# Up-projection of a layer started on the scaled residual, before the root of its norm is known

## The reference

```
x = x + merged @ w_out[l]
h = rms_norm(x, norm_ffn[l])              # x * rsqrt(mean(x*x) + EPS) * gain
ff_g, ff_u = jnp.split(h @ ffn_up[l], 2, axis=-1)
ff_g = causal_dwconv(ff_g, ffn_conv_w[l], ffn_conv_b[l])      # three taps along the tokens
x = x + (jax.nn.gelu(ff_g) * ff_u) @ ffn_down[l]
```

## Time and profile before

| | us |
|---|---|
| median of three runs | 3583.91 (3582.96 to 3587.26) |
| the profiled execution, its own time | 3586.41 |
| its span, first to last instruction | 3584.6 |
| PE busy | 3518.6 |
| DVE busy | 2136.5 |
| ACT busy | 1397.5 |

### The profile page before, as it was taken

One profiled execution on the slowest core, in us unless ns is written; L12 is line 12 of the kernel. 1 busy time (PEld: TensorE's weight loads), 2 busy tenths in 40 slices (PEclk: granted clock), 3 DMA queues, 4 the chain that ended last, 5 costly groups with the idle time before them and its releaser, 6 DMA issues. The chain is left out here.

```text
span 3584.6 us, 53211 instructions
## 1 busy us (share of the span) xinstructions
PE 3518.6 (98%) x21547; PEld 2874.6 (80%) x21547; DVE 2136.5 (60%) x3001; ACT 1397.5 (39%) x1599; POOL 0.2 (0%) x4
## 2 busy tenths in 40 slices
PE   8999999999999999999999999999999999999998
PEld 6778778887877787788878778988888778878887
DVE  6888565876368885658763657653233667652233
ACT  6465433433254554334432334233222443332223
POOL 0000000000000000000000000000000000000000
PEclk9999999999999999999999999999999999999999
DMA  4222222554232222225542331132222330133321
GB/s 130 80 83 60 83 94 98 197 197 154 88 93 75 76 66 83 94 95 200 196 155 84 94 129 49 50 107 94 94 94 86 103 129 26 61 106 98 101 94 70
DMA packets 273304, 364.38 MB, mean 102 GB/s; under 512 B 22637, under 2 KB 218977, under 8 KB 271841
## 3 DMA queue, kind: packets, MB, share of 16 engines
q1 hardware_dynamic: 247856, 311.34, 27.2%
q10 hardware_dynamic: 25264, 50.43, 4.0%
HBM read 351.79 MB, written 9.96 MB: 101 GB/s over the span
## 5 line engine op out<-in xcount | busy, mean ns | idle before, releaser
L249 PE MATMUL banks<-act_hi,w_hi 128*128 128x512 f32 x4064 | 1607.8, 396 | 21.8 <-issue 6.1
L251 PE MATMUL banks<-act_hi,w_lo 128*128 128x512 f32 x4064 | 1584.4, 390 | 0.0
L250 PE MATMUL banks<-act_lo,w_hi 128*128 128x512 f32 x4064 | 1583.4, 390 | 0.0
L171 DVE TENSOR_TENSOR w_lo<-w_raw,w_hi 128x2048 fp32r<-128x2048 f32 (+1 forms) x280 | 629.1, 2247 | 637.9 <-ACT w_hi L165 633.4
L249 PEld LDWEIGHTS banks<-act_hi,w_hi 128*128 128x128 f32 x4064 | 763.3, 188 | 217.6 <-issue 46.7
L251 PEld LDWEIGHTS banks<-act_hi,w_lo 128*128 128x128 f32 x4064 | 762.5, 188 | 162.3
L250 PEld LDWEIGHTS banks<-act_lo,w_hi 128*128 128x128 f32 x4064 | 763.2, 188 | 158.8 <-issue 3.8
L165 ACT ACTIVATE w_hi<-w_raw 128x2048 fp32r<-128x2048 f32 (+1 forms) x280 | 526.5, 1881 | 909.5 <-PE banks L251 845.8
L2127 DVE SCALAR_TENSOR_TENSOR arena<-arena,small 128x512 f32<-128x512 f32 x168 | 126.3, 752 | 12.9
L249 PE MATMUL banks<-w_hi,act_hi 128*128 128x256 f32 x384 | 111.0, 289 | 3.6 <-DVE w_lo L171 3.6
L250 PE MATMUL banks<-w_lo,act_hi 128*128 128x256 f32 x384 | 109.3, 285 | 0.0
(11 more groups left out here) (388 smaller groups left out, 3385.1 us busy)
## 6 DMA issues: line engine op xcount, KB each, us to landing
w_raw<-in_w_in SPq DMA_DIRECT2D x98, 1024.0 KB, 5.5
w_raw<-in_ffn_up SPq DMA_DIRECT2D x48, 1024.0 KB, 5.4
arena<-in_ada_w ACTq DMA_DIRECT2D x24, 2048.0 KB, 8.1
w_raw<-in_w_gu SPq DMA_DIRECT2D x44, 1024.0 KB, 5.1
w_raw<-in_ffn_down SPq DMA_DIRECT2D x24, 1024.0 KB, 5.0
w_raw<-in_w_down SPq DMA_DIRECT2D x20, 1024.0 KB, 4.9
w_raw<-in_w_out SPq DMA_DIRECT2D x16, 1024.0 KB, 4.9
w_raw<-in_w_branch SPq DMA_DIRECT2D x12, 1024.0 KB, 5.0
```

The source lines that it names most:

```text
L171: self.core.nc.vector.tensor_tensor(view(self.lo[:, s]), view(self.raw[:, s]), view(self.hi[:, s]).bitcast(FP32), ALU.subtract)\
L249: nc.tensor.matmul(out, wh, ah, start=first, stop=False)
L250: nc.tensor.matmul(out, wh, al, start=False, stop=False)
L251: return nc.tensor.matmul(out, wl, ah, start=False, stop=last)
```

## The change

- **Outer.plain** takes the place of norm behind w_out. While w_out's last slot runs, each tile is added to x, ACT rounds x * gain (without the root) into act_hi in the order of the banks (4, 5, 6, 7, 0, 1, 2, 3), DVE makes the rest, and ACT squares x. The eight squares are now added up wholly on DVE (seven additions, six_dve with j = 3 added), and PE sums one slot instead of three.
- **pe_first_plain** runs pair 0 over these operands, step by step in that order, with the sum behind slot 1's first step and the spreading behind its third. ACT copies the spread root out of bank 6 (root_wide). **pe_second_plain** runs pair 1 over the same operands. The turn-over matmuls are gone.
- The results of pairs 0 and 1 are multiplied by root_wide where they leave their banks (rooted_pads, rooted_values), now on DVE; the gelu is multiplied in behind (gated).
- During pair 1 DVE computes the 8 normalised operands (normalised) and ACT rounds each one as soon as pair 1's bank 3 has used the old one (spent); pair 2's first bank waits for each rest (ready). From pair 2 on all is as before, with the operands in the new order.
- **conditions**: chunks 0 and 1 of the modulation are summed on DVE ahead of the two slots of w_out's last pair; they are loaded during the merge (chunk 0 into arena tiles 0 to 7, chunk 1 into the hidden tiles). Chunk 11 is loaded in pair 2 into tiles of its own (8 to 15), and summed right behind pair 10. The chunks 2 to 10 stay in their pairs.
- At the end w_lo of the down-projection comes ahead of the last convolution, the down-projection's first operand ahead of both products, and its first slot goes over the banks in the order 0, 1, 6, 7, 2, 3, 4, 5, with the fold ahead of bank 6.

```diff
@@ six_dve
-        elif j == 1:
+        elif j in (1, 3):
@@ Kernel
+    def pe_first_plain(self, pe, u, n, order, sums, spread):
...
+            pe.wait_ge(ring.split[s], u + 1)
+            for at, k in enumerate(order):
+                if s == 0:
+                    pe.wait_ge(n.hi, at + 1)
+                for t in (0, 1):
+                    b, cols = 2 * s + t, slice(t * P, t * P + P)
+                    if at == 0:
+                        pe.wait_ge(n.x, order.index(b) + 1)
+                    nc.tensor.matmul(self.ps[:, b, :], wh[:, k, cols], hi[:, at, :], start=(at == 0), stop=False)
+                    nc.tensor.matmul(self.ps[:, b, :], wl[:, k, cols], hi[:, at, :], start=False, stop=False)
+                if s == 0:
+                    pe.wait_ge(n.lo, at + 1)
...
+                if s == 1 and at == 0:
+                    sums(pe)
+                if s == 1 and at == 2:
+                    spread(pe)
@@ merge, act_part
+            if conditions is not None:
+                act.wait_ge(y_lo, n_br - first_made)
+                conditions.load(act, 0)
             self.schedule.hi(act, u + n_br, 0)
...
             self.schedule.hi(act, u + n_br, 1)
+            if conditions is not None:
+                act.wait_ge(core.sem("ada_in"), 16)
+                conditions.load(act, 1)
@@ Outer.plain
+        def sums(pe):
+            pe.wait_ge(n.pair, 7)
+            k.sum_slot(pe, n, 0, True, True).then_inc(n.summed, 1)
+        def act_part(act):
+            self.act(act)
+            k.schedule.hi(act, last_u, 0)
+            for i, m in enumerate(self.order):
+                act.wait_ge(n.x, i + 1)
+                if i == KD - 2:
+                    act.wait_ge(k.ring.done[1], last_u)
+                k.nc.scalar.activation(k.hi[:, i, :], k.x[:, m, :], ACT.Copy, scale=gain(m)).then_inc(n.hi, 1)
+                if i == KD - 2:
+                    k.schedule.hi(act, last_u, 1)
+                k.square_act(act, n, i, m)
+            k.schedule.hi(act, last_u + 1, 0)
+            k.root_act(act, n)
+            act.wait_ge(n.spread, 1)
+            k.nc.scalar.activation(root_wide, k.ps[:, 6, :], ACT.Copy).then_inc(root_ok, 1)
+        def dve_part(dve):
...
+            conditions.add(dve, 0)
+            self.slot_dve(dve, 1, 0)
+            conditions.add(dve, 1)
+            self.slot_dve(dve, 1, 1)
+            for i in range(KD):
+                self.add_dve(dve, i)
+                if i == 0:
+                    k.schedule.lo(dve, last_u, 0)
+                else:
+                    lo_of(i - 1)
+                if i in (3, 5):
+                    k.six_dve(dve, n, i // 2 - 1)
+            lo_of(KD - 1)
+            k.schedule.lo(dve, last_u, 1)
+            k.six_dve(dve, n, 2)
+            k.six_dve(dve, n, 3)
+            self.free_banks(dve)
+            k.rstd_dve(dve, n)
+            k.schedule.lo(dve, last_u + 1, 0)
@@ ffn_up, pe_part
-            self.pe_first(pe, u, n)
-            with pe.Fori(1, LAST) as i:
-                self.pe_feature(pe, i + u)
-            self.pe_feature(pe, u + LAST, spent, between)
-            fold().then_inc(mod_ps, 1)
+            self.pe_first_plain(pe, u, n, order, add_up, spread)
+            self.pe_second_plain(pe, u + 1, order, spent)
+            self.pe_feature(pe, u + 2, order=order, ready=n.lo)
+            with pe.Fori(3, LAST) as i:
+                self.pe_feature(pe, i + u, order=order)
+            self.pe_feature(pe, u + LAST, spent, between, order=order)
@@ ffn_up, act_part
+            act.wait_ge(ada_used, 3)
+            conditions.load(act, 2)
+            gelu(act, 0)
+            self.schedule.hi(act, u + 2, 0)
+            for at in range(KD):
+                act.wait_ge(n.normed, at + 1)
...
+                nc.scalar.activation(self.hi[:, at, :], normed[at], ACT.Copy).then_inc(n.hi, 1)
+            self.schedule.hi(act, u + 2, 1)
+            gelu(act, 1)
+            act.wait_ge(n.lo, 2 * KD)
+            act.wait_ge(self.core.sem("ada_in"), 48)
+            conditions.load(act, LAST)
@@ ffn_up, dve_part
+            dve.wait_ge(root_ok, 1)
+            rooted_pads(0)
+            conv(0)
+            rooted_values(0)
+            self.schedule.lo(dve, u + 1, 1)
+            dve.drain()
+            gated(0)
+            normalised()
+            rooted_pads(1)
+            self.schedule.lo(dve, u + 2, 0)
+            lower(0, 4)
+            conv(1)
+            lower(4, KD)
+            rooted_values(1)
+            self.schedule.lo(dve, u + 2, 1)
+            dve.drain()
+            gated(1)
...
-            condition(LAST).then_inc(mod_sums, 1)
+            condition(dve, LAST).then_inc(mod_sums, 1)
+            self.schedule.lo(dve, u + LAST + 1, 0)
             conv(LAST)
-            self.schedule.lo(dve, u + LAST + 1, 0)
-            product(LAST, 0)
-            for s in (0, 1):
-                down.lo(dve, 0, s)
-            product(LAST, 1)
+            down.lo(dve, 0, 0)
+            for t in (0, 1):
+                product(LAST, t)
+            down.lo(dve, 0, 1)
...
+            elif m == 6:
+                fold(pe)
+        down.bank_ready, down.first_order = bank_ready, (0, 1, 6, 7, 2, 3, 4, 5)
```

More of the change, by code:

```diff
@@ L127 @@
 MergeParts = namedtuple("MergeParts", "pe act dve bank_ready first_done")
+PlainParts = namedtuple("PlainParts", "n gain order sums spread root_wide root_ok")
+Conditions = namedtuple("Conditions", "load add sums")
 NormSems = namedtuple("NormSems", "x squared pair summed mean root rstd spread normed hi lo")
@@ L355, in param, with pe_feature @@
         return self.cols[:, buf, row:row + n]
-    def pe_feature(self, pe, u, spent=None, between=None, done=0):
+    def pe_feature(self, pe, u, spent=None, between=None, done=0, order=range(KD), ready=None):
         ring, hi, lo = self.ring, self.hi, self.lo
@@ new lines, in pe_second_plain @@
+    def pe_second_plain(self, pe, u, order, spent):
+        ring, hi, lo = self.ring, self.hi, self.lo
+        for s in (0, 1):
+            wh = ring.hi[:, s].rearrange("p (k n) -> p k n", k=8)
+            wl = ring.lo[:, s].rearrange("p (k n) -> p k n", k=8)
+            steps = [(at, t) for at in range(KD) for t in (0, 1)]
+            if s == 0:
+                steps.sort(key=lambda step: step[1])
+            pe.wait_ge(ring.split[s], u + 1)
+            for at, t in steps:
+                b, k, cols = 2 * s + t, order[at], slice(t * P, t * P + P)
+                if at == 0:
+                    pe.wait_ge(ring.bank_free[b], u)
+                last = three_pass(self.nc, self.ps[:, b, :], (wh[:, k, cols], wl[:, k, cols]),
+                                  (hi[:, at, :], lo[:, at, :]), at == 0, at == KD - 1)
+                if at == KD - 1:
+                    last.then_inc(ring.done[s] if t else ring.tile[s], 1)
+                elif s == 1 and t == 1:
+                    last.then_inc(spent, 1)
@@ L706, in __init__ @@
         self.order = [4, 5, 6, 7, 0, 1, 2, 3]
+        self.first_order = range(KD)
         self.x_ready = None
@@ L743, in slot_pe @@
             op = self.base + 2 * s + kk
-            for m in range(KD):
+            for m in (self.first_order if first and kk == 0 else range(KD)):
                 if first and kk == 0:
@@ L2050, in ffn_up @@
+    def ffn_up(self, late, conditions, mod_at, params, down):
+        n, gain, order, add_up, spread, root_wide, root_ok = late
+        sums, condition = conditions.sums, conditions.add
+        ada_used, mod_ps, mod_ok, mod_sums = (self.core.sem("ada_used"), self.core.sem("mod_ps"),
+                                              self.core.sem("mod_ok"), self.core.sem("mod_sums"))
+        normed = [self.arena[:, a, :] for a in range(8, 16)]
         nc, core, ring, ps, A = self.nc, self.core, self.ring, self.ps, self.arena
@@ new lines, in pe_part, with fold @@
+            self.pe_feature(pe, u + 2, order=order, ready=n.lo)
+            with pe.Fori(3, LAST) as i:
+                self.pe_feature(pe, i + u, order=order)
+            self.pe_feature(pe, u + LAST, spent, between, order=order)
+        def fold(pe):
+            pe.wait_ge(mod_sums, 1)
+            columns = sums.rearrange("p (c r) -> p r c", r=4)
+            for r in range(4):
+                for half in (0, 1):
+                    last = nc.tensor.matmul(ps[32 * r:32 * r + 32, 4, 0:48],
+                                            self.c("ident2")[:, 32 * half:32 * half + 32], columns[:, r, :],
+                                            start=(half == 0), stop=(half == 1))
+            last.then_inc(mod_ps, 1)
@@ L2120, in conv @@
                     ins.then_inc(conv_ok, 1)
[L2122 to L2135, removed]
             def product(i, t):
@@ L2197, in front @@
         params = nxt.params()
-        up = self.ffn_up(out.n, ada, mod_at, params, self.down)
+        up = self.ffn_up(late, conditions, mod_at, params, self.down)
         early = self.down.early()
```

149 lines of the change are left out of this document (114 added, 35 removed).

## The result

| | before | after |
|---|---|---|
| median of the runs, us | 3583.43 (3581.37 to 3587.26, 4 runs) | 3561.57 (3558.67 to 3563.30, 4 runs) |
| the profiled execution | 3586.41 | 3563.06 |
| its span | 3584.6 | 3561.3 |

The ratio is 0.9937, with a 95% interval of 0.9920 to 0.9954: 21.9 us faster, where 24.6 were forecast, and 3561.6 against a predicted 3559. A second set of runs of the same kernel gave 3558.70 (3557.34 to 3561.67, 5 runs) against 3583.99, ratio 0.9932 (0.9918 to 0.9945): 25.3 us.

A forecast was written before the change was run, and what follows sets the result against it. PE, busy for 98% of the span, was taken as the bound. Gains of 12.8 and 11.8 us in the two layers, together 24.6, plus 2.8 of clock loss, off the profiled 3586.41 gave 3559 us; range 3553 to 3569.

The forecast's parts named there:

- Change 1: Pairs 0 and 1 over the unnormalised residual: PE loses the norm's 9.76 us and two w_lo waits, 0.63 and 1.24.
- hand layout of DVE: DVE's steps timed from w_out's last slot (t = 0): last double addition ends at 23.2, PE waits 0.3 us.
- eighth margin: Pair 2's eighth operand: last low part at about 60.8, asked for at 61.7, margin 0.9 us.
- The table load: On ACT ahead of the root: costs 1.28 us without the skill's 1.38 us drain; PE doesn't wait for the reciprocal.
- Change 2: Chunks 0 and 1 of the modulation summed during w_out: w_lo starts 0.4 us late, cost 0.
- room: Moving the chunk sums, 7.86 us of DVE each, out of pairs 0 and 1 makes room for the plain pairs.
- Change 3: Early chunk 11, fold and bank order at the up-projection's end: of the 3.52 us gap 0.56 stay.
- The sum: Stretch from w_out to down-projection 264.5 us: layers gain 12.8 and 11.8, together 24.6, plus 2.8 for the clock.
- (a): Thin handover margins leak in pair 2, at the sum and ahead of the down-projection: 10 us, 3569; chance 20%.
- (b): Clock falls in the new gap round the sum or spreading: 3 us each, 3562 to 3565; chance 12%.
- (c): Chunk 1's load lands late ahead of w_out's last w_lo, PE waits; 3591 at 35 us landing; chance 2%.
- (d): Norm stage hidden by an equal wait for weights in the up-projection's pair 0: within 3 us of 3581; chance 3%.

The follow-up runs named there:

- chunks_late: The changed kernel with the sums of modulation chunks 0 and 1 back in pairs 0 and 1: 3575.67 us, ratio 0.9975 to the kernel before.
- after_again: The changed kernel once more with no edit: 3558.70 us (3557.34 to 3561.67).
- sum_first: The changed kernel with the sum of squares ahead of slot 1's first step instead of behind it: 3561.07 us, ratio 0.9933 to the kernel before.
- after_late_11: The changed kernel with chunk 11 loaded in pair 11 again, new order kept: 3566.34 us, ratio 0.9948 to the kernel before.
- before_early_11: The kernel before with chunk 11 of the modulation loaded at the head of the up-projection: 3595.24 us, ratio 1.0032.
- before_11_in_pair_1: The kernel before with chunk 11 of the modulation loaded in pair 1, behind w_hi of pair 2: 3574.79 us, ratio 0.9969.

## Why the prediction was right, and where it was off

**Change 1** was right in size and mechanism. Forecast length of a stretch 264.5, measured 263.9 in both layers. The hand layout of DVE placed the last pair addition at t = 23.2, measured 22.9, so the wait of 0.3 us for the sum wasn't there. The sum and the spreading cost 0.81 + 0.1 each, against 1.08 and 1.05. The last w_lo of slot 1 was forecast at 20.3 and ended at 20.1. The eighth margin in pair 2 was put at 0.9 and is 1.6 us: the last low part came 1.3 us sooner than laid out (640.29, t = 59.45, against 60.8), and PE asks 0.7 sooner (641.88, t = 61.04, against 61.7), since sum, wait and spreading took less.

**The table load.** The rows before and after agree that the load starts right behind the activation ahead of it, 0.01 and 0.02 us. In the changed kernel the root starts 0.02 us behind the load; in the kernel before it starts 0.81 behind it, at 597.75, and waits for DVE's mean meanwhile. The Trainium skill (ScalarE: Activation LUTs, What ACT_TABLE_LOAD costs) adds a drain of about 1.38 us to each switch; the changed kernel shows one on neither side of the load, and in the kernel before the 0.81 leaves no room for it. PE did not wait for the reciprocal.

**Change 2** cost nothing, as forecast: slot 1's w_lo of w_out starts at 572.38, t = -8.5, against t = -8.7 before; 0.4 later was forecast, and it is 0.2. What the forecast called room is shown by chunks_late: 8.0 to 8.6 us in each layer.

**Change 3** had the right sum and a cause named too broadly. The forecast took 3 us of each gap away for the early data and for the order together, and did not use DVE's wait of 3.18 us for these data. The runs give it all to the data: the old order with early data is as fast (3558.59 against 3558.70), and the new order with late data keeps 2.3 and 2.8 us of the 3.0.

**The sum.** The profiled pair of stretches gained 13.4 and 12.4 us, 25.8 against the forecast 24.6, and the clock loss of 2.8 behind layer 2's gap was gone. That would be 28.6 for the profiled executions, and they differ by 23.3. The missing 5 us lie outside the stretches. The program ahead of them and between them took 2.8 us less than before, and what stands behind the stretch of layer 2 took 8.0 us more: there 34 us ran at half clock (17 before), and the 2 us at 2190 come on top. In the second profile (after_again) that part took 0.6 us more, and 27.7 of the 28.6 arrived. In the medians the forecast gain of 24.6 stands between 21.9 and 25.3. That it comes so near is partly luck: each stretch gained 0.6 more than forecast, and the part behind, which the forecast held to be unchanged, lost 0.6 to 8.0 us.

**Rivals.** (a) None of the margins leaked; PE has no wait in the stretch. (b) The clock fell at neither the sum nor the spreading, in either layer, and not even over 2 us in sum_first. It did fall behind a wait of 2.6 us (after_late_11, layer 2) and in the waits of 3.9 us (chunks_late, both layers), and did not behind 2.15 us in layer 1 of after_late_11. In the kernel before it fell in layer 2's wait of 2.91 us and not in layer 1's of 2.97. So the length of the wait alone doesn't settle it. The forecast's price of 3 us a fall holds: 2.8 in the kernel before, 2.9 and 2.6 in chunks_late. (c) Chunk 1 landed in time. That its mechanism is real, and where it bites, before_early_11 shows with 8.7 us. (d) falls with the stretch itself.

**Left open.** Why the clock falls near 2195 us in some executions was not tried further: no kernel here changes the second model. Whether the changed program itself costs time there stays open too. From an instruction of PE in layer 2's down-projection (1840.7 us in the changed kernel, 1872.1 in the kernel before) to its last, the three profiles of the kernel before and its variants take 1702.9 to 1705.2 us, the seven of the changed kernel and its variants 1704.6 to 1711.9. The share of the plain pass alone was not run by itself. What is left when before_11_in_pair_1's 10.6 us are taken from the 25 of the changed kernel is some 14 us, 7 for each layer; by the stretches it is 8.3 and 7.9 (272.2 and 271.7 against 263.9), and 10.4 and 9.4 if the falls in the gap of the norm are as long as in the kernel before.

## What to carry to other kernels

A norm's scale per token commutes with the product behind it, so the product can begin on the unscaled operand, while the sum of squares, root and spreading run beside it; the price is a scaling of the results on another engine, and that engine must have the room for it, which may first have to be made by moving other work away. When a gap stands behind a chain of an in-order engine, look for a load that the chain waits for before you reorder the chain. A load that is moved earlier must not be put right in front of one that is needed sooner.

## What was not expected of the hardware

A 2 MB load put directly ahead of another one raised DVE's wait from 1.5 to 8.6 us, and made the kernel slower than before by 0.32% although it removed 3 us in each layer elsewhere. One of the slots of weights beside it was late too: ACT waited 4.4 us for it. The time at half clock in one and the same kernel varied from 30.8 to 37.4 us in three profiles, at changing places, which is up to 3.3 us of the time: about the distance between the two medians of the changed kernel, 2.9. And 2516 instructions of PE in the second model, which the change doesn't touch, took 104.4 us in three profiles with the old first model and 106.1 to 106.6 in three with the new one, all at full clock.
